# One table of 8 KB rows for U and V, copied in DRAM beside the weight loads, and one gather for both rows of a choice

## The chip, the cores and the metric

One core of a Trainium2 chip runs the whole program. The metric is the device time of one execution in microseconds (us), the median of several runs. Everything is fp32.

## The reference, cut to what matters

A first block of two layers (feed-forward, a mixer, feed-forward each) works on 256 tokens of width 1024; then a second block: an attention mixer, and a feed-forward that picks experts for every token. Only the last part is changed:

```
q = (hc @ w_query)                                # 1024 -> 8 heads x 2 x 128
s = einsum('bthpd,hpnd->bthpn', q, sub_keys)      # scores against 2 x 128 sub-keys of a head
s_top, i_top = top_k(s, 16)
g_s, pos = top_k(all 16 x 16 sums, 16)            # 16 experts of 16384 for each head and token
e_idx = ...                                       # 8 heads x 16 = 128 choices per token
u = u_emb[e_idx]                                  # rows of 1024 floats (4 KB)
act = gelu(einsum('btd,bthkd->bthk', hc, u))
out = einsum('bthk,bthkd->btd', softmax(g_s) * act, v_emb[e_idx])
```

So each of 256 tokens takes 128 rows of U and the same 128 rows of V, 4 KB each: 268.4 MB in all. U and V are inputs of 64 MiB each.

## The kernel before, in words

The order of all work is written out by hand, one program for each engine, with semaphores between them.

**Weights.** Up to the last matrix (`wq`), every weight matrix is streamed in chunks of 2 MiB through two slots of `WR`. SP issues the loads: `load` (L447 on), and for the middle of each feed-forward's `up` matrix the loop in `load_up` (L477). A load waits until DVE has split the last half of the chunk two before it (`lo_ready`). ScalarE (L1293, L1302) copies a half into `WH`, VectorE (L1766, L1781) writes the remainder into `WL`, and TensorE makes three products of each weight. The phases are, in order: up00, down00, kv0, kv1, pool_in, group, pool_outx, pool_out, up01, down01, up10, down10, diff_in, diff_out, up11, down11, in2, out2, wq. GpSimd (POOL) meanwhile loads the 24 MiB matrix `w_ada` in 48 pieces of 512 KB (L529) and reduces them.

**Choices.** VectorE makes the top-16 lists (`choose`, `subkeys`, `gates`) for 16 choices of 128 tokens at a time and signals `index_ready`. Its code interleaves this with the experts' products for the first 128 tokens.

**Experts.** 128 tokens lie on the 128 partitions. The 128 choices of a tile of tokens are 32 groups of `NG` = 4 choices; two tiles give 64 groups. For each group n:

- POOL gathers the four U rows (`gather_u`, L628 on), and the four V rows (`gather_v`, L637 on), with one indirect DMA (L624) per choice and table: 128 rows of 4 KB, 512 KB. Its order is U of group n+1, then V of group n. All four gathers of a group and table count on one semaphore.
- DVE waits for the whole U set, makes four dot products with the token's activations (L2350), then waits for ACT's gelu and multiplies with the gates (L2357).
- ACT makes gelu (L1699) and four diagonal matrices (L1704), double buffered: the diagonals of group n wait for `v_used` of group n-2.
- PE waits for the diagonals and the V set and adds diagonal times V rows in PSUM (L1247), two products for each choice; the last product of a group signals `v_used`.

There are four sets of buffers for U and four for V (`ring`, L100). Two of each (`late_*`) lie over the weight buffers and can be used from group `EARLY` = 6 on, once the last weights are used. U's set comes free with `dots_ready`, V's with `v_used` of the group that used it before. Most of the second tile runs in a hardware loop of four groups.

## Time and profile before

| | |
|---|---|
| median of 3 runs | 2057.4 us (2057.3 to 2062.47) |
| the profiled execution: its own time | 2055.95 us |
| its span, first to last instruction | 2054.4 us |
| busy: PE, DVE, POOL, ACT | 86%, 61%, 44%, 39% of the span |
| moved by DMA | 515.8 MB |
| first gather issued | 1276.8 us from the start |

The busy shares are over the whole span. Up to some 1277 us the weights are streamed, and from there the gathers run; the two parts must be read apart. DMA share in a view is the mean busy share of the core's 16 DMA engines; it can come out a few per cent over 1.

### The profile page before, as it was taken

The page shows a single profiled execution, that of the slowest core. Times are in us where ns is not written, and L with a number is a line of the kernel's source. Part 1 is how long each engine was busy: PE and PEld are TensorE (multiplying, and loading weights), DVE is VectorE, ACT ScalarE, POOL GpSimd, SP SyncE. Part 2 cuts the span into 40 slices and gives each one's busy share as a digit, 9 for nine tenths or more (in the row PEclk, how much of TensorE's full clock was granted, in tenths as well). Part 3 has the DMA queues.
Part 4 walks back from the last instruction along what each step waited for, and adds up shares of the span by engine and source line. Part 5 has one row for each costly group of instructions (what it writes and reads, how often), then busy time and mean ns, then how long its engine had stood idle before and what let it go on. Part 6 is the DMA issues. An engine that isn't in the chain of part 4 may idle for free.

```text
span 2054.4 us, 22931 instructions
## 1 busy us (share of the span) xinstructions
PE 1765.3 (86%) x8110; PEld 1305.6 (64%) x8110; DVE 1261.8 (61%) x2212; ACT 797.1 (39%) x1423; POOL 896.7 (44%) x858
## 2 busy tenths in 40 slices
PE   7999999999999999999989987875675687767677
PEld 6888998888888889888879867642232233223233
DVE  4658756555566567666565847775867776443433
ACT  5444444544544356654443564321222322111112
POOL 5545600362055410115440211556666666666663
PEclk9999999999999999999998998886988799878788
DMA  7775644675576563357563442988999999999995
GB/s 238 247 278 203 213 136 164 205 235 193 184 229 225 195 204 132 139 186 244 205 210 119 151 142 88 348 314 335 373 358 356 355 371 392 374 361 385 355 387 216
DMA packets 248396, 515.80 MB, mean 251 GB/s; under 512 B 16065, under 2 KB 157682, under 8 KB 248306
## 3 DMA queue, kind: packets, MB, share of 16 engines
q0 software_dynamic: 83168, 301.54, 39.7%
q1 hardware_dynamic: 164466, 211.92, 30.8%
q10 hardware_dynamic: 672, 1.18, 0.2%
q8 instruction: 53, 0.87, 0.2%
q14 instruction: 37, 0.30, 0.0%
HBM read 509.34 MB, written 5.26 MB: 250 GB/s over the span
## 4 chain that ended last, share of the span: by engine, by line
PE 62%; issue 25%; DVE 6%; ACT 3%; another core or an unknown queue 2%; DMA 2%; SPq 0%; ACTq 0%; DVEq 0%
PE P L1247 9%; PE PX L789 8%; PE PX L791 8%; PE PX L790 7%; PE P L706 5%; PE P L708 5%; PE P L707 5%; PE P L655 2%; PE P L656 2%; PE P L657 2%; DVE WL L1766 1%; PE P L694 1%; PE P L695 1%; PE P L696 1%
## 5 line engine op out<-in xcount | busy, mean ns | idle before, releaser
L1766 DVE TENSOR_TENSOR WL<-WR,WH 128x1024 fp32r<-128x1024 f32 (+1 forms) x246 | 321.8, 1349 | 191.6 <-ACT WH L1293 191.5
L1293 ACT ACTIVATE WH<-WR 128x1024 fp32r<-128x1024 f32 (+1 forms) x272 | 271.0, 1044 | 324.5 <-PE P L708 150.0
L1247 PE MATMUL P<-early_v,M 128*128 128x512 f32 x544 | 269.0, 653 | 113.3 <-issue 68.6
L1247 PE MATMUL P<-late_v,M 128*128 128x512 f32 x480 | 239.5, 659 | 101.7 <-ACT M L1704 54.8
L789 PE MATMUL PX<-WH,hTh 128*128 128x512 f32 x704 | 279.8, 397 | 5.0 <-DVE WL L1774 4.7
L1247 PEld LDWEIGHTS P<-early_v,M 128*128 128x128 f32 x544 | 112.3, 210 | 265.3 <-issue 218.9
L791 PE MATMUL PX<-WH,hTl 128*128 128x512 f32 x704 | 275.8, 392 | 0.0
L790 PE MATMUL PX<-WL,hTh 128*128 128x512 f32 x704 | 275.0, 391 | 0.0
L1781 DVE TENSOR_TENSOR WL<-WR,WH 128x1024 fp32r<-128x1024 f32 x128 | 177.3, 1426 | 132.0 <-ACT WH L1302 132.0
L1247 PEld LDWEIGHTS P<-late_v,M 128*128 128x128 f32 x480 | 100.6, 213 | 238.8 <-issue 177.2
L624 POOL DMA_INDIRECT early_u<-in_peer_u,M x136 | 131.4, 966 | 152.5 <-DVE M L1989 84.1
L531 POOL TENSOR_TENSOR adaW<-adaW,silc 128x1024 f32<-128x1024 f32 x48 | 100.1, 2086 | 216.4 <-DMA adaW<-in_w_ada 216.4
L1302 ACT ACTIVATE WH<-WR 128x1024 fp32r<-128x1024 f32 x128 | 128.7, 1052 | 159.0 <-PE PX L791 159.0
L706 PE MATMUL P<-WH,actH 128*128 128x512 f32 x472 | 186.6, 395 | 2.0 <-DVE actL L1903 1.0
L708 PE MATMUL P<-WH,actL 128*128 128x512 f32 x472 | 184.1, 390 | 0.0
L707 PE MATMUL P<-WL,actH 128*128 128x512 f32 x472 | 183.8, 389 | 0.0
L1704 ACT ACTIVATE M<-ident,lam 128x128 f32<-128x128 f32 x256 | 81.8, 389 | 260.2 <-remote 190.8
L2350 DVE CUSTOM_DVE_ANT_0 early_u<-early_u,PX 128x1024 f32<-128x1024 f32 x136 | 158.0, 1217 | 25.9 <-DMA early_u<-in_peer_u,M 13.6
L624 POOL DMA_INDIRECT early_v<-in_peer_v,M x136 | 128.9, 948 | 69.2 <-issue 38.7
L789 PEld LDWEIGHTS PX<-WH,hTh 128*128 128x128 f32 x704 | 132.9, 189 | 32.5 <-issue 6.5
L791 PEld LDWEIGHTS PX<-WH,hTl 128*128 128x128 f32 x704 | 132.7, 188 | 28.6
L790 PEld LDWEIGHTS PX<-WL,hTh 128*128 128x128 f32 x704 | 133.0, 189 | 26.7
(367 smaller groups left out, 3330.2 us busy)
## 6 DMA issues: line engine op xcount, KB each, us to landing
WR<-in_ffn_w_up SPq DMA_DIRECT2D x88, 1024.0 KB, 7.4
WR<-in_ffn_w_down SPq DMA_DIRECT2D x44, 1024.0 KB, 6.1
adaW<-in_w_ada POOLq DMA_DIRECT2D x48, 512.0 KB, 4.8
WR<-in_diff_w_in SPq DMA_DIRECT2D x14, 1024.0 KB, 6.9
WR<-in_w_in SPq DMA_DIRECT2D x13, 1024.0 KB, 6.9
WR<-in_mem_w_kv SPq DMA_DIRECT2D x8, 1024.0 KB, 6.7
WR<-in_peer_wq SPq DMA_DIRECT2D x8, 1024.0 KB, 7.3
WR<-in_pool_w_in SPq DMA_DIRECT2D x6, 1024.0 KB, 6.3
```

The source lines that it names most:

```text
L624: pool.indirect_dma_start(rows[:, i, :], None, table, bass.IndirectOffsetOnAxis(ap=eidx[:, at:at + 1], axis=0)).then_inc(landed[i], 16)
L706: mm(o, xh, WH[:, U % 2, w], start=first and kk == 0, stop=False)
L707: mm(o, xh, WL[:, U % 2, w], start=False, stop=False)
L708: return mm(o, xl, WH[:, U % 2, w], start=False, stop=last_half and kk == 1)
L789: mm(o, xh, WH[:, u, w], start=(k == 0), stop=False)
L790: mm(o, xh, WL[:, u, w], start=False, stop=False)
L791: return mm(o, xl, WH[:, u, w], start=False, stop=(k == KT - 1))
L1247: last = mm(P[2 * t + q][:], diag[:, n % 2, i], rows_v(n)[:, i, q * 512:q * 512 + 512], start=n % GROUPS == 0 and i == 0, stop=n % GROUPS ...
L1293: nc.scalar.activation(split_view(WH, U % 2, kind, part), raw(c % 2, kind, h, part), copy)\
L1766: tt(split_view(WL, U % 2, kind, part), raw(c % 2, kind, h, part), split_view(WH, U % 2, kind, part).bitcast(F32), ALU.subtract)\
L1781: tt(split_view(WL, U % 2, "pair", part), raw(c % 2, "pair", h, part), split_view(WH, U % 2, "pair", part).bitcast(F32), ALU.subtract).the ...
L2350: last = nc.vector.tensor_tensor_reduce(out=u[:, i], in0=u[:, i], in1=HTOK[n // GROUPS], scale=1.0, scalar=0.0, op0=ALU.mult, op1=ALU.add, ...
```

## The change

A table `uv_rows` of 16384 rows of 8 KB is made in DRAM, with row e = U's row e, then V's row e. SP copies it there from the two inputs, 128 or 256 rows at a time (one DMA for U, one for V), issued after a chunk's weight loads, in the same queue. Every POOL gather then takes 8 KB rows. The buffers `u` and `v` become one ring of four sets of four choices; each choice has a landing semaphore of its own, and `v_used` counts choices, so that the next gather into a choice's buffer can go once that choice's products are done.

```
+    uv_rows = nc.dram_tensor("uv_rows", (128 * 128, 2 * D), F32, kind="Internal").ap()
+    COPIES = dict(kv0=(1, 1), kv1=(1, 1), pool_in=(1, 1, 1), group=(1,), pool_outx=(1,), pool_out=(1, 1), diff_in=(2,) * 7,
+                  diff_out=(1, 1, 1), in2=(1,) * 7, up00=(0, 0, 0), up01=(1, 1, 1), up10=(1, 1, 1), up11=(1, 1, 1),
+                  down00=(2, 1) * 3, down01=(2, 1) * 3, down10=(2, 1) * 3, down11=(2, 1) * 3)
+    IN_LOOP = (1, 2)
...
+        def copy_rows(at, n):
+
+            for q, table in enumerate((a["peer_u_2"][0], a["peer_v_2"][0])):
+                sp.dma_start(uv_rows[bass.ds(at, n), q * D:q * D + D], table[bass.ds(at, n), :]).then_inc(S["uv_copied"], 16)
+
+        def copy_chunk(name, c):
+
+            n = COPIES.get(name, ())
+            if c < len(n) and n[c]:
+                copy_rows(copy_from[name] + 128 * sum(n[:c]), 128 * n[c])
...
                 load(p["C"] + c)
+                copy_chunk(f"up{i}{f}", c)
...
+                    copy_rows(r * (128 * sum(IN_LOOP)) + (loop_from + 128 * sum(IN_LOOP[:j])), 128 * IN_LOOP[j])
...
+        def gather(n):
+            call = ALL_CALLS.index((n // GROUPS, n % GROUPS * NG // 16))
+            pool.wait_ge(S["index_ready"], call + 1)
+            if n == EARLY:
+                pool.wait_ge(S["half_used"], len(half_of))
             for i in range(NG):
                 at = n * NG + i
...
+                if user_before(n) is not None:
+                    pool.wait_ge(S["v_used"], NG * user_before(n) + i + 1)
+                pool.indirect_dma_start(rows_uv(n)[:, i, :], None, uv_rows,
+                                        bass.IndirectOffsetOnAxis(ap=eidx[:, at:at + 1], axis=0)).then_inc(uv_landed[ring(n)][i], 16)
...
-        gather_u(0)
+        pool.wait_ge(S["uv_copied"], UV_COPIED)
         for n in range(2 * GROUPS):
-            if n + 1 < 2 * GROUPS:
-                gather_u(n + 1)
-            gather_v(n)
+            gather(n)
...
             pe.wait_ge(S["diag_ready"], r * 4 + (n + 1))
-            if n < LAST:
-                pe.wait_ge(v_landed[ring(n)], r * (16 * NG) + turn(n) * 16 * NG)
...
-            last.then_inc(S["v_used"], 1)
+                last.then_inc(S["v_used"], 1)
...
-                act.wait_ge(S["v_used"], r * 4 + (n - 1))
+                act.wait_ge(S["v_used"], r * (4 * NG) + NG * (n - 1))
...
             for i in range(NG):
-                last = nc.vector.tensor_tensor_reduce(out=u[:, i], in0=u[:, i], in1=HTOK[n // GROUPS], scale=1.0, scalar=0.0,
+                dve.wait_ge(uv_landed[ring(n)][i], r * 16 + 16 * turn(n))
+                last = nc.vector.tensor_tensor_reduce(out=u[:, i, 0:D], in0=u[:, i, 0:D], in1=HTOK[n // GROUPS], scale=1.0, scalar=0.0,
                                                       op0=ALU.mult, op1=ALU.add, accum_out=dots[:, g, i:i + 1])
```

`COPIES` gives, for each chunk of a phase, how many times 128 rows are copied behind its load; `IN_LOOP` does so for the eight chunks of an `up` phase's loop. Together they cover the 16384 rows. Phases out2 and wq have none.

## Rows read from the trace of the kernel before

**Rows 1.** The page's 40 slices of 51 us each, TensorE and DMA
```profile
PE   7999999999999999999989987875675687767677
...
DMA  7775644675576563357563442988999999999995
```

**Rows 2.** Waits by engine and line, from 0 to 1277 us
```profile
engine line waited for: us in total, times, longest us
...
DVE WL L1766 <- ACT WH L1293: 186.4, 97, 7.0
ACT WH L1302 <- PE PX L791: 159.0, 64, 3.2
```

**Rows 3.** Busy time by stretch: up00, down00, up01, down01, up10, down10, diff_in, up11, down11, wq
```profile
core 0: us, PE busy (x) PEld busy (x) DVE busy (x) ACT busy (x) POOL busy (x), PEclk, DMA share, GB/s
...
35.00:126.00 91.00, 91.00 (x418) 75.27 (x417) 56.92 (x58) 44.81 (x59) 53.18 (x39) 1.00 0.73 236
126.00:190.00 64.00, 63.01 (x292) 52.08 (x291) 46.74 (x44) 29.20 (x36) 29.24 (x26) 1.00 0.70 256
352.00:463.00 111.00, 110.91 (x512) 91.52 (x512) 68.57 (x77) 58.36 (x79) 48.80 (x40) 1.00 0.68 211
463.00:526.00 63.00, 63.00 (x293) 52.39 (x292) 32.93 (x33) 25.39 (x29) 10.43 (x7) 1.00 0.52 192
530.00:642.00 112.00, 111.88 (x515) 92.34 (x514) 70.58 (x78) 56.94 (x76) 43.33 (x31) 1.00 0.69 221
642.00:703.00 61.00, 61.00 (x286) 50.72 (x285) 36.18 (x34) 26.81 (x32) 25.37 (x18) 1.00 0.61 217
720.00:812.00 92.00, 90.25 (x673) 84.00 (x672) 60.50 (x91) 53.96 (x106) 9.77 (x7) 1.00 0.50 161
892.00:1004.00 112.00, 112.00 (x513) 92.64 (x512) 66.81 (x69) 53.90 (x70) 54.91 (x39) 1.00 0.72 231
1004.00:1055.00 51.00, 51.00 (x238) 42.49 (x237) 28.89 (x24) 19.90 (x22) 24.89 (x18) 1.00 0.59 214
...
1172.00:1277.00 105.00, 85.02 (x607) 75.44 (x605) 62.62 (x110) 54.20 (x114) 13.42 (x18) 0.95 0.37 122
```

**Rows 4.** The same view, three stretches of the gathers
```profile
1277.00:1500.00 223.00, 159.46 (x542) 90.31 (x543) 161.76 (x502) 58.83 (x131) 137.58 (x143) 0.82 0.90 337
1500.00:1740.00 240.00, 168.56 (x347) 70.43 (x345) 175.72 (x463) 58.61 (x140) 157.93 (x168) 0.87 0.96 367
1740.00:2020.00 280.00, 193.19 (x386) 82.24 (x387) 121.68 (x228) 35.89 (x127) 184.96 (x197) 0.80 0.96 370
```

**Rows 5.** Timeline of POOL, 1900 to 1908 us: start, duration, what, idle before
```profile
1900.58 0.94 POOL L624 DMA_INDIRECT early_u<-in_peer_u,M  x1 [0.30 <-issue]
1905.99 0.94 POOL L624 DMA_INDIRECT early_v<-in_peer_v,M  x1 [4.48 <-remote]
1907.24 0.94 POOL L624 DMA_INDIRECT early_v<-in_peer_v,M  x1 [0.30 <-issue]
```

**Rows 6.** Timeline of ACT at the same place
```profile
1905.82 1.28 ACT L1704 ACTIVATE M<-ident,lam 128x128 f32<-128x128 f32 x4 [21.40 <-remote]
```

**Rows 7.** Timeline of PE: the products of one group
```profile
1907.22 16.73 PE L1247 MATMUL P<-late_v,M 128*128 128x512 f32 x32 [10.54 <-issue]
1923.79 7.03 PE L1247 MATMUL P<-early_v,M 128*128 128x512 f32 x16
```

**Rows 8.** Busy time by stretch: one cycle of 34 us, and a dense part of it
```profile
1906.00:1940.00 34.00, 23.60 (x48) 10.11 (x48) 14.45 (x27) 4.18 (x16) 22.57 (x24) 0.80 0.97 369
1930.00:1939.00 9.00, 0.82 (x2) 0.00 (x0) 0.00 (x0) 0.00 (x0) 4.36 (x5) 0.68 1.03 410
```

**Rows 9.** The page's DMA queues: packets, MB, share of 16 engines' span
```profile
q0 software_dynamic: 83168, 301.54, 39.7%
q1 hardware_dynamic: 164466, 211.92, 30.8%
```

**Rows 10.** Busy time by stretch: the one large write to DRAM in progress
```profile
130.00:140.00 10.00, 10.00 (x48) 8.27 (x47) 5.66 (x7) 3.78 (x6) 0.17 (x1) 1.00 1.01 383
```

**Rows 11.** One line's instructions: L477, issues of weight loads on SP (ns min/median/max)
```profile
L477 SPq DMA_DIRECT2D WR<-in_ffn_w_up x64: 372/410/484, 35.5 to 979.9; - x64
```

**Rows 12.** One line's instructions: L2350, the dot products on DVE
```profile
L2350 DVE CUSTOM_DVE_ANT_0 early_u<-early_u,PX x136: 1211/1216/1222, 1290.8 to 2013.1; 128x1024 f32<-128x1024 f32 x136
```

More of the change, by code:

```diff
@@ L89, in program @@
     stage_a.close()
[L91 to L92 removed]
+    late_uv = sb("late_uv", [128, 2, NG, 2 * D])
     late_h = sb("late_h", [128, 2, D])
@@ L96, in program, with rows_uv @@
     htok1 = sb("htok1", [128, D])
[L97 to L98 removed]
+    early_uv = sb("early_uv", [128, 2, NG, 2 * D])
     def ring(n):
         return n % 2 if n < EARLY else n % 4
[L103 to L107 removed]
+    def rows_uv(n):
+        return early_uv[:, ring(n)] if ring(n) < 2 else late_uv[:, ring(n) - 2]
     def turn(n):
@@ L218, in program @@
     raw_landed = [sem("raw_landed0"), sem("raw_landed1")]
-    u_landed = [sem(f"u_landed{i}") for i in range(4)]
-    v_landed = [sem(f"v_landed{i}") for i in range(4)]
-    LAST = 2 * GROUPS - 2
-    last_landed = [[sem(f"last_landed{g}{i}") for i in range(NG)] for g in range(2)]
+    uv_landed = [[sem(f"uv_landed{g}{i}") for i in range(NG)] for g in range(4)]
     b_landed = [sem("b_landed0"), sem("b_landed1")]
@@ L320, in program @@
         slot_loads.append(total[c % 2])
+    COPIES = dict(kv0=(1, 1), kv1=(1, 1), pool_in=(1, 1, 1), group=(1,), pool_outx=(1,), pool_out=(1, 1), diff_in=(2,) * 7,
+                  diff_out=(1, 1, 1), in2=(1,) * 7, up00=(0, 0, 0), up01=(1, 1, 1), up10=(1, 1, 1), up11=(1, 1, 1),
+                  down00=(2, 1) * 3, down01=(2, 1) * 3, down10=(2, 1) * 3, down11=(2, 1) * 3)
+    IN_LOOP = (1, 2)
+    copy_from, copies, at = {}, 0, 0
+    for name in phases:
+        copy_from[name] = at
+        at += 128 * sum(COPIES.get(name, ()))
+        copies += sum(n > 0 for n in COPIES.get(name, ()))
+        if name.startswith("up"):
+            at += 4 * 128 * sum(IN_LOOP)
+            copies += 4 * len(IN_LOOP)
+    assert at == 128 * 128
+    UV_COPIED = 2 * 16 * copies
     block = ctx.enter_context(nc.Block())
@@ L462, in raw_dst_of @@
             return raw_dst(slot, kind, part)
+        def copy_rows(at, n):
[5 more added lines that the diff above has]
+                copy_rows(copy_from[name] + 128 * sum(n[:c]), 128 * n[c])
         def load_up(i, f):
             p = phases[f"up{i}{f}"]
+            loop_from = copy_from[f"up{i}{f}"] + 128 * sum(COPIES[f"up{i}{f}"])
             for c in range(3):
                 load(p["C"] + c)
+                copy_chunk(f"up{i}{f}", c)
                 if i == f == 0 and c == 1:
@@ L483, in _ @@
             else:
-                for c in range(p["C"], p["C"] + p["nc"]):
-                    load(c)
+                for c in range(p["nc"]):
+                    load(p["C"] + c)
+                    copy_chunk(name, c)
         sp.wait_ge(S["index_ready"], len(ALL_CALLS))
@@ L1240, in experts @@
             pe.wait_ge(S["diag_ready"], r * 4 + (n + 1))
-            if n < LAST:
-                pe.wait_ge(v_landed[ring(n)], r * (16 * NG) + turn(n) * 16 * NG)
             for i in range(NG):
-                if n >= LAST:
-                    pe.wait_ge(last_landed[n - LAST][i], 16)
                 for q in range(2):
-                    last = mm(P[2 * t + q][:], diag[:, n % 2, i], rows_v(n)[:, i, q * 512:q * 512 + 512],
+                    last = mm(P[2 * t + q][:], diag[:, n % 2, i], rows_uv(n)[:, i, D + q * 512:D + q * 512 + 512],
                               start=n % GROUPS == 0 and i == 0, stop=n % GROUPS == GROUPS - 1 and i == NG - 1, skip_group_check=True)
-            last.then_inc(S["v_used"], 1)
+                last.then_inc(S["v_used"], 1)
         for j in range(8):
@@ L2385, in add_experts @@
         def add_experts(t):
-            dve.wait_ge(S["v_used"], t * GROUPS + GROUPS)
+            dve.wait_ge(S["v_used"], NG * (t * GROUPS + GROUPS))
             if t:
```

29 lines of the change are left out of this document (2 added, 27 removed).

## The prediction, made before the changed kernel ran

> **What bounds the kernel now.** I read the page's slices first [rows 1]. They show two programs in one. Up to about the 25th slice (1277 us) TensorE's digit is 9 nearly everywhere while DMA's lies between 3 and 7; after it DMA's is 8 or 9 and TensorE's 5 to 7. The waits of the first part [rows 2] say the same: the splitting engines wait for each other and, in the end, for TensorE to free a buffer; no wait for a weight load stands high. So weights arrive early, and TensorE sets the pace. In the second part the stretches [rows 4] show DMA at a share of 0.90, 0.96 and 0.96, moving 337, 367 and 370 GB/s. The gathers set the end.
>
> How much is left there? The timeline from 1900 us on shows a cycle. POOL issues gathers every 1.245 us (0.94 and 0.30 idle), then stops once for 4.48 us [rows 5]; ACT, which needs the same count `v_used` for its diagonals, stands 21.4 us and is released at the same moment [rows 6]; PE idles 10.54 us [rows 7]. One cycle is 34 us and three groups, 24 gathers [rows 8]: 24 x 1.245 + 4.48 = 34.4. In the dense part the engines move 410 GB/s at a share of 1.03, over the cycle 369 [rows 8]. So a tenth of the rate is lost after each stop. POOL cannot make it good: 524 KB in 1.245 us is 421 GB/s, hardly more than the 410 that DMA takes. Why the count comes so late the trace doesn't say.
>
> **The copies.** They move 128 x 2 x 512 KiB = 134.2 MB. COPIES and IN_LOOP make 93 calls, so 186 more DMAs on SP, in its queue between weight loads. At the 0.41 us of a load's issue [rows 11] that is 76 us of SP, which otherwise only waits for slots; on a chunk's path stand two issues, 0.8 us, before the wait for the next slot. TensorE's time for a chunk is about 11 us (112 us of a stretch with some ten chunks, [rows 3]), so SP hides it. What counts is the data: a load queues behind the copy that was issued before it.
>
> What does a byte copied from DRAM to DRAM cost? No such transfer of any size is in the trace. The nearest rows from one side: a gather reads DRAM at 410 GB/s and share 1.03 [rows 8], the store of `rel_rows` writes to DRAM among loads at 383 GB/s in total and share 1.01 [rows 10]. If a DMA engine reads and writes at once, the copy costs what a gather costs: 398 GB/s per unit of share. From the other side: if reading and writing DRAM take turns, each byte costs twice, 199. No reason excludes either; I take the first, since a gather too is a read and a write in each packet and the rows of either direction are near each other. The range keeps both.
>
> Room is (1.03 minus share) times length, stretch by stretch [rows 3], against the copies' need at 398:
> - up00: 27.3 us of room, 12.6 MB need 31.6, over by 4.3. down00: 21.1, 9.4 MB need 23.7, over by 2.6.
> - up01: 38.9, 15.7 MB need 39.5: 0.6. down01: 32.1, need 23.7: none.
> - up10: 38.1: 1.4. down10: 25.6: none. diff_in: 48.8, 14.7 MB need 36.9: none.
> - up11: 34.7: 4.8. down11: 22.4: 1.3.
>
> Sum 15 us. The other phases have room. For copies that come in lumps of 1 and 2 MiB (2.6 and 5.3 us) before a load, I add 0.1 us for each of the 68 feed-forward chunks: 22 us in all. The wait of gather 0 for the copies costs nothing: after in2 comes wq without copies, 105 us at share 0.37 [rows 3]. If the copies ran beyond that, every gather would be late.
>
> The Trainium skill has a rule that speaks against this. "DMA: Bandwidth & Descriptors", section "Latency and other measured facts", gives 214 GB/s per direction as the full rate of copies between tensors in HBM. By that figure, an estimate, the copies would take 627 us of all engines, near the second case above; no run here shows it yet.
>
> **The gathers.** Bytes stay 268.4 MB; 512 gathers become 256.
> - *Packets.* q0 took 0.397 x 16 x 2054.4 / 83168 = 156.9 ns per packet of 3626 bytes, q1 61.6 ns per 1288 bytes [rows 9]. A straight line through both has 9.1 ns per packet. 32768 packets fewer on 16 engines: 18.6 us. I take 18. The other bound is nothing, if a row of 8 KB is cut in two. The same page of the Trainium skill, section "SWDGE vs HWDGE vs iDMA", wants packets of at most 4096 bytes; by that rule these 18 us would be gone.
> - *POOL.* At 0.94 + 0.30 us for an instruction of 1 MB it could issue 842 GB/s, and refill the queues after a stop. If a row makes two descriptors, an instruction may cost 2.5 us, and POOL stays at 421: then this gain is nothing.
> - *Late stretch*, 1740 to 2020: at 410 instead of 370, 280 x (1 - 370/410) = 27. I take 20, since the late count's cause isn't known and may remain; the bounds are 0 and 27.
> - *Middle*, 1500 to 1740: 240 x (1 - 367/410) = 25. DVE is busy 73% there with the choices of the second tile, and buffers come free only behind it. I take half, 13; bounds 0 and 25.
> - *Early*, 1277 to 1500: 40 us are lost at 337 GB/s, but two sets of buffers until wq ends and the first top lists make that, and both stay. I take 4; bounds 0 and 15.
>
> The buffers are the same bytes. U's set was free after the dot products, now it waits for PE: against that each choice is freed alone. DVE now waits for each choice, and the sorting of later choices is queued behind that wait; the dots of a group take 4 x 1.22 = 4.9 us [rows 12] of 10.2 us that 4 MB need at 410 GB/s. PE needs 7.03 us for a group [rows 7], also under 10.2. PE's own wait for V goes, since the diagonal comes from the same landing. These edits cost nothing while DMA is the slower one. The end, from the last landing on, is one dot, gelu, diagonals and seven us of PE as before: nothing.
>
> Gain 18 + 20 + 13 + 4 = 55. Against the profiled execution's own 2055.95 us: + 22 - 55 = 2023. The median of the runs is 1.5 us above it: 2024.
>
> **The rivals.**
> - *The copies starve TensorE.* Place: the queue of SP in the up and down phases. With 199 GB/s the needs double: over by 36, 26, 40, 15, 41, 22, 25, 44 and 25 us in the order above, 275 together, less 55: about 2277. At 300 GB/s at share 1.03 (reads and writes hinder each other in part) I get 97, so 2099. It decides from where the overload passes 55 us, some 330 GB/s. For it: no free room in four up phases even at the best rate. Against it: TensorE has two halves split ahead, and `w_ada`'s loads can give way. The result is slower.
> - *The gathers gain little.* If the rate is what DRAM gives for scattered rows and rows of 8 KB are cut, and the late counts remain, 0 to 15 us are won and 15 to 22 paid: about 2063. For it: 410 is seen as a ceiling everywhere. Against: the loss of a tenth is plain in the cycle.
> - *More is won.* With POOL far ahead the early and middle stretches also reach 410 and the copies cost nothing: 2055.95 - 18 - 27 - 25 - 15, about 1973.
> - *It doesn't do what it says:* the table isn't complete at 1277 and gather 0 waits. This is part of the first rival, since FIFO order makes the last copies late only if the loads are late too.
>
> **Chances.** Forecast 0.42. Copies starve TensorE: 0.37, of it 0.19 near half rate and 0.18 between. Gathers gain little 0.15, of it 0.07 within 0.3%, 0.06 slower and 0.02 faster. More is won 0.06. That makes faster 0.50, same 0.07, slower 0.43; 0.3% (6 us) is about what a measurement of this kernel can tell from no change. The likeliest case's own range is 1990 to 2050. For 8 in 10 the range reaches from 1975 up to 2200: it leaves out the worst of the copies at about half rate, some 0.15, and a little below. It is wide since cases of both signs hold most of the chance.
>
> **What the profile would show.** TensorE at 9 up to 1277 us with DMA near full in the up phases, and gather 0 still near 1277 to 1300: the copies' step is right. Waits of ACT for DMA of `WR` of more than 30 us in total, or a first gather after 1340: the first rival. In the gathers: 256 instructions of about 0.94 us on POOL, with long waits for buffers between them, and a rate near 410 GB/s in the last stretch. Packets of q0 down by about 32768 prove rows of one packet; if they stay, the 18 us are wrong. ACT's waits of 20 us gone: the late count was tied to the old waits. If they stay and the rate still rises, the refill did it. The prediction is wrong if copies run below 330 GB/s or the rate of the gathers stays below 385.

## The result, and the profile after

The changed kernel takes 2008.15 us (median of 4 runs, 1992.75 to 2009.55) against 2058.89 (4 runs of the kernel before, 2057.3 to 2062.47) in the same comparison: ratio 0.9729, interval 0.9707 to 0.9752. That is faster by 51 us, well beyond the 6 us that a measurement can tell from nothing. The forecast said 2024. On another chip (e6 below) the same change is slower than the kernel before, by 28 us; so this number belongs to the chip that it was measured on.

The profiled execution took 2008.95 us with a span of 2007.4 (before: 2055.95 and 2054.4). One instant splits it in two: the first gather starts at 1320.40, where it was 1276.8. Up to there the change costs 43.6 us. From there to the end of the span it takes 687.0 us instead of 777.6, and wins 90.6. The net of the two is the 47 us between the spans. The forecast had 22 and 55.

The page of the changed kernel, its slices of 50 us (the GB/s row is what moved in each):

```profile
PE   7999999999999999999999789788688877778776
...
DMA  8999976799899989758998656368999999999995
GB/s 268 326 373 381 305 257 252 261 348 373 290 313 347 373 282 337 259 206 306 330 335 300 201 193 204 105 256 328 420 420 420 420 420 419 420 421 421 421 421 224
```

DMA's digit, 2 to 7 before the gathers [rows 1], is mostly 7 to 9 now where copies run, while TensorE keeps its 9 in most slices. From the 29th slice on the rate stands at 419 to 421 GB/s in every slice but the last. That flat row is what the change won: no stop, no slow recovery after one.

The same page, its DMA part: packets by size, the two large queues (packets, MB, share of 16 engines' span), and issues (KB each, median us from issue to landing):

```profile
DMA packets 247274, 649.99 MB, mean 324 GB/s; under 512 B 14945, under 2 KB 156562, under 8 KB 214418
...
q1 hardware_dynamic: 200210, 346.15, 50.4%
q0 software_dynamic: 46304, 301.52, 37.6%
...
WR<-in_ffn_w_up SPq DMA_DIRECT2D x88, 1024.0 KB, 9.9
WR<-in_ffn_w_down SPq DMA_DIRECT2D x44, 1024.0 KB, 11.1
uv_rows<-in_peer_u SPq DMA_DIRECT2D x35, 1024.0 KB, 13.5
```

- q0 fell from 83168 packets [rows 9] to 46304, by 36864: 32768 for the rows, and 16 small ones for each of the 256 gathers that are gone. Of all packets 247274 - 214418 = 32856 have 8 KB or more: each gathered row of 8 KB went as one packet.
- q1 grew by 35744 packets and 134.2 MB, the copies. The time of all its packets grew by 0.504 x 16 x 2007.4 - 0.308 x 16 x 2054.4 = 6063 us, so 170 ns for a packet of 3755 bytes: with 16 engines 354 GB/s. That puts the whole growth down to the copies. Against the 398 GB/s of a gather [rows 8] a copied byte costs an eighth more, not double.
- A load of `w_up` lands after 9.9 us and one of `w_down` after 11.1. In the trace of the kernel before these were 7.4 and 6.1.

Busy time by stretch, changed kernel (columns as in [rows 3]; the stretches are those of [rows 3] and [rows 4], five of the feed-forward phases and three of the gathers, the last one ended before the drain):

```profile
126.00:190.00 64.00, 60.97 (x280) 49.77 (x279) 40.35 (x41) 26.63 (x33) 23.47 (x23) 1.00 1.00 384
463.00:526.00 63.00, 60.32 (x272) 49.35 (x271) 34.80 (x34) 24.87 (x31) 21.86 (x16) 0.97 0.93 343
530.00:642.00 112.00, 111.87 (x512) 92.03 (x511) 68.51 (x75) 55.30 (x73) 29.07 (x21) 1.00 0.98 317
642.00:703.00 61.00, 56.30 (x259) 46.21 (x258) 36.54 (x35) 25.79 (x33) 28.45 (x20) 0.97 1.02 370
892.00:1004.00 112.00, 109.67 (x500) 89.70 (x499) 71.87 (x73) 56.09 (x76) 30.46 (x22) 0.98 0.91 303
1277.00:1500.00 223.00, 175.14 (x755) 113.24 (x754) 184.83 (x550) 74.51 (x159) 66.25 (x68) 0.88 0.82 324
1500.00:1740.00 240.00, 192.56 (x397) 79.99 (x395) 189.35 (x491) 65.21 (x156) 94.58 (x100) 0.91 1.01 420
1740.00:1970.00 230.00, 177.99 (x365) 73.53 (x366) 117.53 (x211) 34.10 (x115) 82.68 (x89) 0.93 1.01 420
```

The middle and the late stretch went from 367 and 370 GB/s to 420, at a share of 1.01 (416 GB/s per unit of share; 4 KB rows gave 398). In up10 TensorE still has 111.87 of 112 us, in up11 109.67 where it had 112.00. In the down phases it idles: 60.32 of 63 us in down01 and 56.30 of 61 in down10, where it had 63.00 and 61.00.

The gathers gain in all their stretches, the first included. By 1500 us the kernel before had moved 73.0 MB of rows, 223 us after its first gather; the changed kernel had them after 194. The last 100 us of that stretch, first of the kernel before, then of the changed one:

```profile
1400.00:1500.00 100.00, 61.30 (x118) 25.66 (x119) 66.82 (x212) 22.24 (x51) 62.44 (x67) 0.80 0.91 347
1400.00:1500.00 100.00, 70.34 (x148) 30.52 (x149) 92.57 (x310) 31.80 (x72) 36.92 (x39) 0.84 1.01 420
```

Waits by engine and line (us in total, times, longest), changed kernel, 0 to 1300 us:

```profile
POOL adaW L554 <- DMA adaW<-in_w_ada: 343.3, 48, 10.1
...
ACT WH L1309 <- DMA WR<-in_ffn_w_up: 64.1, 13, 7.1
...
ACT WH L1300 <- DMA WR<-in_ffn_w_down: 38.0, 9, 6.0
```

No wait for a weight load stood high before [rows 2]. Now ACT stands 64.1 + 38.0 us for `WR` in these two lines, and 145 us over all matrices against 24 before. Part of it reaches TensorE: those are its idle microseconds in the down phases.

The same view from 1300 us on, then POOL's timeline (start, duration, what, idle before and who ended it) and the gathers as one line's instructions (ns min/median/max, first and last start):

```profile
ACT lam L1706 <- DVE lam L2357: 471.8, 64, 9.5
...
POOL early_uv L651 <- PE P L1254: 182.9, 111, 15.2
POOL late_uv L651 <- PE P L1254: 182.2, 108, 7.6
...
DVE early_uv L2357 <- DMA early_uv<-uv_rows,M: 82.3, 69, 3.2
```

```profile
1320.40 1.77 POOL L651 DMA_INDIRECT early_uv<-uv_rows,M  x1 [76.00 <-DVE M L1996]
...
1346.74 0.94 POOL L651 DMA_INDIRECT early_uv<-uv_rows,M  x1 [15.23 <-PE P L1254]
```

```profile
L651 POOL DMA_INDIRECT early_uv<-uv_rows,M x136: 932/936/1768, 1320.4 to 1940.3; - x136
L651 POOL DMA_INDIRECT late_uv<-uv_rows,M x120: 932/936/1183, 1393.5 to 1960.2; - x120
```

256 instructions of 0.936 us issue the 256 gathers of 1 MB, and POOL waits 365 us for buffers in between: it is far ahead of the DMA engines. ACT's single waits of 21.4 us [rows 6] are gone; its longest is 9.5. The first gather waited for DVE's index, not for the copies.

### The profile page after: what moved, and what is told of

It reads as the page before. It is cut to its first block, busy times and chain, and to the rows that moved or that the text cites. A ratio compares the mean times of both kernels' runs of the same rounds, so it can differ in the third digit from the quotient of the medians.

```text
span 2007.4 us, 22993 instructions
## 1 busy us (share of the span) xinstructions
PE 1774.0 (88%) x8110; PEld 1306.8 (65%) x8110; DVE 1277.5 (64%) x2212; ACT 795.6 (40%) x1423; POOL 652.1 (32%) x602
## 2 busy tenths in 40 slices
DMA packets 247274, 649.99 MB, mean 324 GB/s; under 512 B 14945, under 2 KB 156562, under 8 KB 214418
## 3 DMA queue, kind: packets, MB, share of 16 engines
q0 software_dynamic: 46304, 301.52, 37.6%
## 4 chain that ended last, share of the span: by engine, by line
PE 39%; DMA 28%; DVE 16%; POOL 8%; ACT 4%; issue 4%; SPq 0%; ACTq 0%; DVEq 0%; POOLq 0%
DMA late_uv<-uv_rows,M 12%; DMA adaW<-in_w_ada 10%; PE P L1254 6%; PE P L717 3%; PE P L718 3%; PE P L719 3%; PE PX L800 3%; DVE WL L1773 3%; DMA early_uv<-uv_rows,M 3%; PE PX L802 3%; PE PX L801 3%; POOL adaW L554 2%; POOL adaW L555 2%; DVE early_uv L2357 2%; PE P L666 2%
## 5 line engine op out<-in xcount | busy, mean ns | idle before, releaser
L1254 PE MATMUL P<-early_uv,M 128*128 128x512 f32 x544 | 260.4, 635 | 56.2 <-ACT M L1711 56.2
L1254 PE MATMUL P<-late_uv,M 128*128 128x512 f32 x480 | 240.8, 660 | 78.0 <-ACT M L1711 78.0
L1788 DVE TENSOR_TENSOR WL<-WR,WH 128x1024 fp32r<-128x1024 f32 x128 | 185.1, 1486 | 135.8 <-ACT WH L1309 135.7
L1254 PEld LDWEIGHTS P<-late_uv,M 128*128 128x128 f32 x480 | 99.4, 213 | 218.2 <-issue 117.7
L1254 PEld LDWEIGHTS P<-early_uv,M 128*128 128x128 f32 x544 | 108.0, 203 | 204.5 <-issue 133.6
L651 POOL DMA_INDIRECT early_uv<-uv_rows,M x136 | 130.1, 956 | 286.2 <-PE P L1254 182.9
L2357 DVE CUSTOM_DVE_ANT_0 early_uv<-early_uv,PX 128x1024 f32<-128x1024 f32 x136 | 162.5, 1220 | 85.5 <-DMA early_uv<-uv_rows,M 82.3
L1706 ACT ACTIVATE lam<-lam 128x4 f32<-128x4 f32 x64 | 13.1, 205 | 471.8 <-DVE lam L2357 471.8
L2357 DVE CUSTOM_DVE_ANT_0 late_uv<-late_uv,PX 128x1024 f32<-128x1024 f32 x120 | 143.4, 1220 | 76.4 <-DMA late_uv<-uv_rows,M 75.8
L651 POOL DMA_INDIRECT late_uv<-uv_rows,M x120 | 113.4, 945 | 187.1 <-PE P L1254 182.2
## 6 DMA issues: line engine op xcount, KB each, us to landing
WR<-in_ffn_w_down SPq DMA_DIRECT2D x44, 1024.0 KB, 11.1
WR<-in_diff_w_in SPq DMA_DIRECT2D x14, 1024.0 KB, 11.6
```

Source lines behind the costliest of these rows:

```text
L651: pool.indirect_dma_start(rows_uv(n)[:, i, :], None, uv_rows, bass.IndirectOffsetOnAxis(ap=eidx[:, at:at + 1], axis=0)).then_inc(uv_landed ...
L1254: last = mm(P[2 * t + q][:], diag[:, n % 2, i], rows_uv(n)[:, i, D + q * 512:D + q * 512 + 512], start=n % GROUPS == 0 and i == 0, stop=n ...
L1788: tt(split_view(WL, U % 2, "pair", part), raw(c % 2, "pair", h, part), split_view(WH, U % 2, "pair", part).bitcast(F32), ALU.subtract).the ...
L2357: last = nc.vector.tensor_tensor_reduce(out=u[:, i, 0:D], in0=u[:, i, 0:D], in1=HTOK[n // GROUPS], scale=1.0, scalar=0.0, op0=ALU.mult, op ...
```

## The experiments

Questions: what do the copies cost, and where; what of the gathers' gain comes from long rows, from the ring released per choice, and from the vanished stops. The kernels of one series ran on one chip, with the kernel before beside them. The four series ran on four chips, and that turned out to matter most. No chip was used in two of them, so a condition of the chip at that hour is not told from the chip itself; within a series no run of the kernel before was of the other kind.

### First series: e1 to e4, the kernel before at 1979.3 us

The expectations were written against a kernel before of about 2057 us. On this chip it took 1979.3 (17 runs, 1977.26 to 1981.78). So only the ratios and the differences within the series can be read.

**e1_no_copies.** The gathers of 8 KB rows without copies:

```
-    uv_rows = nc.dram_tensor("uv_rows", (128 * 128, 2 * D), F32, kind="Internal").ap()
+    uv_rows = a["peer_u_2"][0].rearrange("(a b) n -> a (b n)", b=2)
     ...
-                sp.dma_start(uv_rows[bass.ds(at, n), q * D:q * D + D], table[bass.ds(at, n), :])...
+                pass
     ...
-        pool.wait_ge(S["uv_copied"], UV_COPIED)
     ...
-            stt(eidx[:, at:at + 16], ps[:, 0], float(128), ps[:, 1], ...
+            stt(eidx[:, at:at + 16], ps[:, 0], float(63), ps[:, 1], ...
```

> The changed kernel without its copies: the gathers take rows of 8 KB from U read as a table of 8192 rows, with indices 63 a + b instead of 128 a + b, so V's half and the output are other numbers, while bytes, row size and waits stay. Theory A (the 44 us by which the first gather comes later, 1320 against 1277, are all the copies' cost, and the gathers don't care where the table came from): first gather near 1277, time near 2008 - 44 = 1964. Theory B (part of the delay comes from the new order of gathers, which wait for PE while only two sets are free): first gather at 1277, but a gather part longer than the 687 us of the changed kernel, time 1970 to 1990.

Measured: 1976.35 us (1972.3 to 1977.8), ratio 0.9981 (0.9972 to 0.9991). First gather at 1278.84, steady rate 420 GB/s, span 1974.1, so 695.3 us of gathers, 8.8 more than in e6 below, where the indices are the true ones. They arise ahead of the 25th gather, the first of group 6, which is issued 82.5 us after the first against 72.8 in e6; what caused them wasn't found. Long rows alone, without any cost for making them, are worth 3 us on this chip. The gain of 90 us that the first comparison showed wasn't there to be won.

**e2_two_gathers.** The changed kernel's ring and its release per choice, but two gathers of 4 KB rows, no copies:

```
-                pool.indirect_dma_start(rows_uv(n)[:, i, :], None, uv_rows, ...)
+                for q, table in enumerate((a["peer_u_2"][0], a["peer_v_2"][0])):
+                    pool.indirect_dma_start(rows_uv(n)[:, i, q * D:q * D + D], None, table, ...)
     ...
-                dve.wait_ge(uv_landed[ring(n)][i], r * 16 + 16 * turn(n))
+                dve.wait_ge(uv_landed[ring(n)][i], r * 32 + 32 * turn(n))
```

> No table and no copies; the ring, the landing count per choice and the release per choice as in the changed kernel, but each choice fetched by two gathers of 4 KB rows, from U and from V. Theory rows (the gathers' gain of 91 us comes from 8 KB rows: one packet instead of two, and a POOL that is far ahead): the gather part stays near the 778 us of before, less only a little, time 2030 to 2055. Theory waits (it comes from the waits per choice, which end the cycle of 34 us): dense gathers at 410 GB/s as in the dense part of before, gather part near 687 x 420/410 = 704, time near 1981.

Measured: 1985.43 us (1984.28 to 1986.96), ratio 1.0034 (1.0023 to 1.0044), at 409 to 410 GB/s from the 29th slice on. First gather 1279.87, span 1984.0, gathers 704.1 us. The ring with its waits costs 6 us here instead of the nothing that I had put down. The loss is at the end, not in the waits for buffers: from the first gather to the last one's issue it takes 660.4 us, in e5 below 659.4, but from there to the end of the span 43.7 against 37.8. The last dot product and the last products of TensorE, first of e5 (the kernel before on a chip of this kind), then of e2:

```profile
1957.12 1.22 DVE L2350 CUSTOM_DVE_ANT_0 late_u<-late_u,PX 128x1024 f32<-128x1024 f32 x1
1955.62 13.90 PE L1247 MATMUL P<-late_v,M 128*128 128x512 f32 x32
```

```profile
1966.02 1.22 DVE L2357 CUSTOM_DVE_ANT_0 late_uv<-late_uv,PX 128x1024 f32<-128x1024 f32 x1 [1.30 <-DMA late_uv<-in_peer_v,M]
1969.23 7.13 PE L1254 MATMUL P<-late_uv,M 128*128 128x512 f32 x16 [1.34 <-ACT M L1711]
```

In e5 the dots of the last group are done while V is still on its way, and TensorE then works without a gap up to 7.6 us before the end of the span. In e2 the last dot itself waits for the last landing, and gelu, diagonals and products stand behind it, again up to 7.6 us before the end.

**e3_group_release.** The changed kernel, but the dots start when all four choices of a group have landed, and POOL waits for a whole group's buffers:

```
-                if user_before(n) is not None:
-                    pool.wait_ge(S["v_used"], NG * user_before(n) + i + 1)
+                if i == 0 and user_before(n) is not None:
+                    pool.wait_ge(S["v_used"], NG * user_before(n) + NG)
     ...
                 dve.wait_ge(uv_landed[ring(n)][i], r * 16 + 16 * turn(n))
+            for i in range(NG):
```

> The changed kernel with its table, but buffers released by the group (the first gather of a group waits for all four choices of the group before) and dot products that start when all four rows have landed. Theory rows: no difference, time 2005 to 2012, as the queue is deep enough. Theory waits: the cycle with a drained queue comes back at least in part, 2025 to 2050.

Measured: 2021.21 us (2016.23 to 2025.17), ratio 1.0212 (1.0191 to 1.0234). The changed kernel itself took 2006.8 on another chip of the same kind (e6, below). So the release per choice and the dots per choice, which this run takes away together, are worth some 14 us; its rate from 1500 us on is 418 to 420 GB/s either way, and the loss is ahead of 1500 us, where two sets of buffers have to do (308 GB/s from 1277 to 1500, against 335 in e6).

**e4_copies_only.** The kernel before with all the copies, which nothing reads but a wait for their count ahead of the first gather. The added lines are those of the change (`COPIES`, `copy_rows`, `copy_chunk` and their calls) and

```
+        pool.wait_ge(S["uv_copied"], UV_COPIED)
         gather_u(0)
```

> The kernel before with the copies into the table, which nobody reads; the gathers are those of before and wait for the copies as in the changed kernel. If the copies alone cost what the later first gather shows: first gather near 1320, time near 2058 + 44 = 2102. If the copies only cost together with the new gathers, less.

Measured: 2016.28 us (2014.14 to 2022.34), ratio 1.0197 (1.018 to 1.0215). First gather at 1312.58, which is 32.7 us after that of e2 on the same chip. Copies alone cost 37 us. They are a cost of the weight part; the gathers then run at 408 to 410 GB/s, as without them.

### Second series: e5 to e8, the kernel before at 1978.8 us

Was the first series' chip odd, and does the change lose there? The two kernels as they are, e2 again, and a first remedy for the copies.

**e5_before_again.** No edit.

> The kernel before, unchanged, beside which the first experiments ran at 1979 us on their chip, 79 us below the 2058 of the comparison. Theory chip (the cycle of 34 us with its 21 us waits for v_used appears on some chips only): a profile either with the cycle and about 2058, or without it, gathers steady at 409 GB/s, and about 1979. Theory drift (it is a passing condition of one execution): runs of both kinds in one series.

Measured: 1979.36 us (1977.42 to 1981.22), ratio 1.0003 (0.9994 to 1.0013). Its page, the rate by slice, and two stretches of [rows 4] (columns as there):

```profile
GB/s 239 250 282 192 206 157 171 181 216 236 171 212 220 199 223 171 128 144 203 247 209 213 86 161 144 82 360 369 409 409 409 409 409 409 410 410 410 409 410 262
```

```profile
1277.00:1500.00 223.00, 180.17 (x609) 98.58 (x609) 198.11 (x605) 68.56 (x155) 156.14 (x163) 0.90 0.98 378
1500.00:1740.00 240.00, 186.01 (x369) 76.39 (x368) 164.84 (x411) 57.83 (x145) 181.80 (x192) 0.89 1.03 409
```

It is the same program as in the rows ahead of the prediction. The weight part takes the same time (first gather 1279.87 against 1276.8). But the cycle of [rows 8] isn't there: 409 GB/s all along instead of 367 and 370, and the gathers take 697.2 us instead of 777.6. The 80 us between the chips are the cycle, which holds from the start of the gathers: 378 against 337 GB/s up to 1500 us.

**e6_after_again.** No edit to the changed kernel.

> The changed kernel, unchanged, on the same chip as the kernel before. Theory chip: where the kernel before has the cycle, about 2008 against 2058, ratio 0.973; where it has none (1979), the copies' 40 us stand against some 15 us of faster gathers, so about 2008, ratio 1.012 to 1.017. If instead the gain belongs to the 8 KB rows everywhere, the ratio is 0.973 here too.

Measured: 2006.81 us (2003.14 to 2008.22), ratio 1.0146 (1.0129 to 1.0163): on this chip the change is slower, by 28 us, which is 1.5%, and the interval leaves out 1. First gather 1315.14, span 2001.6, gathers 686.5 us. The changed kernel takes the same time on both kinds of chip (2008.15 and 2006.81); the kernel before doesn't.

**e7_two_gathers_again.** The kernel of e2.

> The ring and the waits per choice, with two gathers of 4 KB rows and no copies, again. On a chip without the cycle 1985 as before. On a chip with the cycle: theory waits (the waits per choice end it) 1985; theory rows (8 KB rows end it) 2040 to 2060.

Measured: 1985.73 us (1983.64 to 1986.81), ratio 1.0036 (1.0022 to 1.0051), as in e2.

**e8_copies_later.** Six units of copies (of 128 rows of U and of V) are moved out of the last two down phases into phases behind, `out2` and `wq` among them:

```
-                  diff_out=(1, 1, 1), in2=(1,) * 7, up00=(0, 0, 0), ...
-                  down00=(2, 1) * 3, down01=(2, 1) * 3, down10=(2, 1) * 3, down11=(2, 1) * 3)
+                  diff_out=(2, 1, 1), in2=(1,) * 7, out2=(1, 1), wq=(1, 1, 1), up00=(0, 0, 0), ...
+                  down00=(2, 1) * 3, down01=(2, 1) * 3, down10=(1,) * 6, down11=(1,) * 6)
```

> The changed kernel with six of the 128 copy units moved out of down10 and down11, the two phases that the changed kernel's trace shows 10 us late each, into diff_out (one), out2 (two) and the first three chunks of wq. Theory room (a phase is late by as much as its copies exceed DMA's room): down10 and down11 late by 3 us each instead of 10, time 10 to 15 us below the changed kernel. Theory backlog (the lateness comes from lumps anywhere): no gain, or the late copies hold up the weights of wq, within 4 us of it.

Measured: 2001.42 us (1996.19 to 2006.08), ratio 1.0108 (1.0082 to 1.0133). From the first load of `down10` to that of the next phase it takes 71.3 us, of `down11` 72.0; in e6 76.9 and 76.9, in e5 68.6 and 68.5. So those phases do pay for their copies, by 8 us each, and a third less copying there takes most of it away. The profiled execution, at 2006.08, is the slowest of the four and shows only 1.7 us of gain at the first gather; the median gains 5.4, where 10 to 15 were expected. down01, whose copies stayed, took 11.7 us more than in e5 (9.1 in e6), and wq with its new copies 3.4 more.

### Third series: e9 and e10, the kernel before at 2057.4 us

Is it the amount of copies in the down phases, or that they come in lumps (2, 1, 2, 1)? This chip has the cycle again.

**e9_downs_light.** All four down phases at one unit a chunk, twelve units moved behind:

```
-                  diff_out=(1, 1, 1), in2=(1,) * 7, up00=(0, 0, 0), ...
-                  down00=(2, 1) * 3, down01=(2, 1) * 3, down10=(2, 1) * 3, down11=(2, 1) * 3)
+                  diff_out=(2, 1, 1), in2=(2,) * 6 + (1,), out2=(1, 1), wq=(1, 1, 1), up00=(0, 0, 0), ...
+                  down00=(1,) * 6, down01=(1,) * 6, down10=(1,) * 6, down11=(1,) * 6)
```

> The changed kernel with one copy unit (1 MiB) behind every chunk of the four down phases instead of 2, 1, 2, 1, 2, 1: twelve units of 128 moved, six of them as before into diff_out, out2 and wq, six more into in2. So far a down phase is 8 to 10 us late with 9 units (3 us with 6), and the up phases hardly. Theory room: four down phases late by about 3 us instead of 8, in2 by 3 us more, first gather near 1295 to 1300 against 1315, time 1988 to 1994. Theory backlog (each unit costs the same wherever it stands): first gather near 1313, time near 2004.

**e10_even_lumps.** The same amount in each down phase as in the change, in even portions of 192 rows:

```
-                  down00=(2, 1) * 3, down01=(2, 1) * 3, down10=(2, 1) * 3, down11=(2, 1) * 3)
+                  down00=(1.5,) * 6, down01=(1.5,) * 6, down10=(1.5,) * 6, down11=(1.5,) * 6)
```

> The changed kernel with the same bytes in every phase, but the down phases' copies even: 1.5 MiB behind each of six chunks instead of 2, 1, 2, 1, 2, 1. Theory lumps (a weight load stands too long behind a copy of 2 MiB): the down phases late by 3 us instead of 8, time near 1990. Theory room (the bytes of a phase count, not their order): no difference, 2004 to 2009.

Measured: e9 1989.24 us (1985.13 to 1993.42), ratio 0.9663 (0.9635 to 0.969); e10 2004.67 us (2002.03 to 2009.43), ratio 0.9744 (0.9712 to 0.9775), about the change's own 0.9729. First gathers 1305.65 and 1317.23. Two down phases, down01 and down10, busy time by stretch, first of e9, then of e10:

```profile
463.00:526.00 63.00, 58.57 (x257) 48.00 (x257) 30.10 (x32) 22.79 (x28) 23.06 (x16) 0.95 0.79 288
642.00:703.00 61.00, 57.74 (x266) 47.52 (x265) 35.15 (x35) 24.45 (x32) 28.57 (x21) 0.97 0.98 342
```

```profile
463.00:526.00 63.00, 58.45 (x263) 47.92 (x262) 30.69 (x33) 23.54 (x28) 24.13 (x16) 0.97 0.88 329
642.00:703.00 61.00, 56.97 (x261) 46.64 (x260) 37.40 (x36) 25.61 (x33) 28.29 (x20) 0.97 1.00 358
```

Even portions change nothing; less in these phases brings the first gather 11.6 us forward, where 15 to 20 were expected. `down01` is no better for it: it moves only 288 GB/s at a share of 0.79, and TensorE is no busier there than in e10.

Where TensorE falls behind can be read by taking the same product of TensorE (the n-th of 8110) in two traces. How much later it starts than in the kernel before (for e6, than in e5), by the time t at which it starts there:

| t in the kernel before, us | 470 | 515 | 660 | 740 | 1000 | 1045 | 1270 |
|---|---|---|---|---|---|---|---|
| changed kernel | 6.2 | 11.0 | 11.3 | 24.4 | 30.2 | 39.2 | 43.0 |
| e6, the same | 5.3 | 13.8 | 13.6 | 24.8 | 24.8 | 31.2 | 34.7 |
| e9 | 5.2 | 13.3 | 13.7 | 21.6 | 21.6 | 25.1 | 28.2 |
| e10 | 5.6 | 12.3 | 12.6 | 24.5 | 24.4 | 36.9 | 39.8 |

From 470 to 515 us TensorE has the end of up01 and the first chunks of down01; from 515 to 660 the rest of down01 and nearly all of up10; from 660 to 740 the entry into down10, down10 and the entry into diff_in; from 1000 to 1045 the entry into down11. These three short stretches hold 26.9, 26.1, 19.5 and 31.1 us of the lag at the end. The rest of down01 and up10, whose chunks have their copies too, cost at most 0.4 us in any of the four. The waits of ACT for a weight load around down01, first of the changed kernel (its third is of 1.11 us, at 497), then all of e9:

```profile
471.82 2.01 ACT L1300 ACTIVATE WH<-WR 128x1024 fp32r<-128x1024 f32 x2 [4.09 <-DMA WR<-in_ffn_w_up]
485.09 2.01 ACT L1300 ACTIVATE WH<-WR 128x1024 fp32r<-128x1024 f32 x2 [5.99 <-DMA WR<-in_ffn_w_down]
```

```profile
470.09 2.01 ACT L1300 ACTIVATE WH<-WR 128x1024 fp32r<-128x1024 f32 x2 [3.32 <-DMA WR<-in_ffn_w_up]
483.94 2.01 ACT L1300 ACTIVATE WH<-WR 128x1024 fp32r<-128x1024 f32 x2 [5.81 <-DMA WR<-in_ffn_w_down]
```

The late loads are those of up01's last chunk and of down01's first. In both kernels these were issued behind the copies of up01's last chunks, which e9 left as they were, and landed 9 to 16 us after their issue; the loads of down01 from the fourth chunk on landed after 5 to 9. Entry and rest of down01, of the changed kernel and of e9:

```profile
470.00:505.00 35.00, 32.32 (x156) 26.39 (x155) 20.33 (x22) 15.06 (x19) 16.17 (x14) 1.00 1.02 388
505.00:535.00 30.00, 30.00 (x127) 24.65 (x126) 10.84 (x11) 9.71 (x10) 1.80 (x2) 0.94 0.81 284
```

```profile
470.00:505.00 35.00, 30.57 (x145) 24.93 (x143) 20.97 (x20) 15.14 (x19) 17.82 (x14) 0.98 0.91 341
505.00:535.00 30.00, 30.00 (x124) 24.74 (x125) 9.71 (x10) 8.05 (x8) 2.31 (x2) 0.91 0.58 213
```

The share of 0.79 is a mean of two stages, 0.91 and 0.58. After its idle time TensorE is busy all the time, but at a granted clock of 0.94 and 0.91, where the kernel before had 1.00 in the same stretch. In the trace these are 3.4 us from 505.4 on and, in e9, 6.8 us from 503.9 on at the lower level (1.2 GHz), with 2.4 GHz around them; so some 2 and 3 us of the lag are the clock. What e9 wins over e10 it wins at the entry into down11 (3.5 us for 12.5) and from 660 to 740 us (7.9 for 11.9). Why nothing comes of it at down01 stays open, and a kernel without copies behind the last chunks of the up phases wasn't run. e9 beats the kernel before, and e10 beside it, on a chip with the cycle. It wasn't run on one without.

### Fourth series: e11 and e12, the kernel before at 2055.8 us

What ends the cycle: the release per choice, the new ring with its waits, or the long rows?

**e11_release_per_choice.** The kernel before, with V's buffers released choice by choice:

```
-        def gathers(rows, table, landed, n):
+        def gathers(rows, table, landed, n, used=False):
             for i in range(NG):
                 at = n * NG + i
+                if used and user_before(n) is not None:
+                    pool.wait_ge(S["v_used"], NG * user_before(n) + i + 1)
     ...
-            last.then_inc(S["v_used"], 1)
+                last.then_inc(S["v_used"], 1)
```

> The kernel before with one edit: v_used is signalled for each choice and V's gathers wait for their own choice; U, the order of the gathers and the landing counts stay. It tells something where the kernel before runs at 2057. Theory release (one late v_used stops POOL and ACT together; counted by the choice it can't): 1980 to 1990. Theory order or landing (the cycle hangs on U before V, or on four gathers that share a count): 2040 to 2057. Where the kernel before runs at 1979, it stays within 5 us of that and tells nothing of the cycle.

Measured: 2071.9 us (2069.57 to 2074.17), ratio 1.0081 (1.006 to 1.0101). Two stretches of e11, and its waits from 1740 to 2000 us:

```profile
1500.00:1740.00 240.00, 158.49 (x323) 66.20 (x322) 168.77 (x452) 53.94 (x129) 149.12 (x159) 0.84 0.92 347
1740.00:2020.00 280.00, 190.69 (x398) 81.13 (x397) 119.45 (x225) 38.31 (x129) 185.60 (x199) 0.84 0.98 373
```

```profile
ACT M L1704 <- remote: 125.2, 7, 25.0
```

The stops stay, with waits of up to 25 us by ACT for `v_used`, and the kernel is 16 us slower than the kernel before. The release alone doesn't end them.

**e12_two_gathers_third.** The kernel of e2 and e7, on a chip with the cycle.

> The changed kernel's ring and waits with two gathers of 4 KB rows and no copies, a third time. It tells something where the kernel before runs at 2057: theory waits (ring and waits per choice alone end the cycle) 1985, so 22 us below the changed kernel; theory rows (only 8 KB rows and the POOL that is far ahead end it) 2040 to 2057.

Measured: 2060.36 us (2057.05 to 2066.84), ratio 1.0023 (1.0008 to 1.0039). Its middle and late stretch and two of its waits from 1740 to 2000 us; then the late stretch of the same kernel in e2, on the chip without the cycle:

```profile
1500.00:1740.00 240.00, 173.01 (x351) 72.38 (x350) 181.67 (x479) 63.62 (x151) 158.62 (x168) 0.86 0.97 366
1740.00:2020.00 280.00, 188.31 (x386) 79.65 (x385) 125.12 (x226) 34.79 (x121) 184.71 (x197) 0.82 0.97 370
```

```profile
ACT lam L1706 <- issue: 96.0, 11, 14.9
...
ACT M L1711 <- remote: 66.5, 5, 14.7
```

```profile
1740.00:1940.00 200.00, 155.08 (x315) 63.16 (x314) 99.27 (x176) 29.65 (x100) 147.44 (x158) 0.92 1.03 410
```

366 and 370 GB/s are, within 1 GB/s, the numbers of [rows 4] again. The kernel is otherwise that of the change: same ring, same waits, same order of work. Only the rows are of 4 KB, from the two inputs, with two instructions for a choice, and there are no copies. So neither the ring nor its waits keep the cycle away; the long rows of the table do, with half as many gather instructions and packets. Row length and number of instructions went together in every kernel here, and weren't told apart. Nor was e1, with 8 KB rows out of an input and no copies, run on a chip with the cycle. That the place of the table in DRAM, or the copies, end the cycle is therefore not excluded; against the copies stands that the last one had landed at 1214 us, 107 us ahead of the first gather.

## Why the prediction was right, and where it was off

The side, the number (2024 for 2008) and the range held, on this chip. The nearness of the number is in part luck: the cost was put 22 us too low and the gain 36 us too low, and the two misses have opposite signs. Point by point:

- **Rate of a copy: right in kind, an eighth too high.** 170 ns per packet of 3755 bytes, 354 GB/s. I had 398 from the gathers. The bound of half that rate is excluded. By the figure that I had quoted from the Trainium skill ("DMA: Bandwidth & Descriptors", "Latency and other measured facts", 214 GB/s per direction) 134 MB would be an estimate of 627 us. The 134.2 MB took 6063 us of packet time, 379 us for each of 16 engines: the measurement doesn't agree, and it decides.
- **Issue of the copies: mis-sized, 76 us for 270.** Each of the 186 issues of copies on SP took longer than a load's 0.41 us, one of them 7.5. The two lines of L475 (ns min/median/max) are these. SP had the time for it in the up phases, which grew by 2.1 us in all in e6 (table below).

```profile
L475 SPq DMA_DIRECT2D uv_rows<-in_peer_u x93: 511/1347/7507, 35.1 to 1202.7; - x93
L475 SPq DMA_DIRECT2D uv_rows<-in_peer_v x93: 522/599/2068, 36.9 to 1203.8; - x93
```

- **Cost of the copies: mis-sized, 22 for 43.6 us.** The step that failed is "down01, down10, diff_in: none". My overloads come to 15.0 us, and 6.8 more were for the chunks' loads behind a copy. Below is by how much each group of phases grew, from the first load of each phase on SP; the last column is e6 less e5, on the chip without the cycle.

| phases | forecast overload | this comparison | e6 less e5 |
|---|---|---|---|
| up00, up01, up10, up11 | 11.1 | 11.1 | 2.1 |
| down00, down01, down10, down11 | 3.9 | 27.1 | 29.7 |
| all others, up to the first gather | 0 | 5.4 | 3.5 |

  The up phases were right, or too dear. The down phases weren't. The first load of a phase is issued some two chunks before TensorE uses it, so a down row also holds the end of the up phase ahead of it. The cost arises there, at the entry into a down phase. Its loads stand behind the last copies of the up phase and the first of its own; in down01 they landed up to 17 us after their issue (the median of all `w_down` loads went from 6.1 to 11.1 us), while a chunk lasts some 10.5 us (63 us, six chunks). The room that I had counted is a mean over the stretch: down01 had 8.4 us of room to spare and still grew by 3.0 us here and by 9.1 in e6. My 0.1 us a chunk for that was far too little. Nor would the measured rate have mended the working: with 354 for 398 the same sums give 41 us, near the 43.6, but 30 of them in the up phases, where 11.1 were measured. e10 excludes the uneven portions as the cause; e8 and e9 say that a third less copying in the down phases gives back 10 us of 16.5 in down10 and down11 (e8), and over all four phases 10 of 27 (e9, against the changed kernel).

- **The wait of gather 0 for the copies: nothing, as forecast.** DVE's index released it after 76.00 us, with the last copy issued before `wq` began.
- **Packets: right.** 32856 packets of 8 KB or more, q0 down by 36864 (the 32768 that I had, and 4096 small ones). At steady state 409.5 became 420 GB/s: 268.4 MB take 639.1 instead of 655.5 us, 16.4 for my 18. From the Trainium skill's preference for packets of at most 4096 bytes ("DMA: Bandwidth & Descriptors", "SWDGE vs HWDGE vs iDMA") I had that these 18 us might be gone; rows of 8 KB went as one packet and were 2.6% faster here.
- **POOL: right.** 0.936 us for an instruction of 1 MB, 365 us of waits for buffers.
- **Late and middle stretch: right in kind, too small.** I took 20 of 27 and half of 25, for fear that the late count stays. It went altogether, and both stretches run at 420, for the same bytes 30 and 34 us less, of which 5 to 6 each are the packets'.
- **Early stretch: wrong.** I took 4 us, with 15 as the bound, since two sets of buffers seemed to make the 337 GB/s. The same 73.0 MB took 29 us less. On the chip without the cycle the kernel before had 378 GB/s there with the same two sets: most of what I had put down to the buffers was the cycle. This stretch has some 20 of the 36 us between 55 and 90.6.
- **Ring and waits "cost nothing", the end "as before": wrong by some 7 us.** e2's gathers take 704.1 us against 697.2 of e5 at the same rate, and 5.9 of the 6.9 lie behind the issue of the last gather: the dots of the last group now wait for the last landing, where U had landed ahead of V. The release per choice, which I had only as a counterweight, is worth at most 14 us, by e3 and with the dots per choice.

The gathers' gain can be told in two parts. On the chip without the cycle it is 697.2 - 686.5 = 10.7 us, of which the steps above make 16.4 - 6.9 = 9.5. What is left of the 90.6, 80 us, is the difference of the kernel before between the two chips, 777.6 - 697.2 = 80.4.

The **rivals**. "The copies starve TensorE" came true in part: ACT's waits for `WR` are 102 us where I had named 30 as the mark, but the rate stayed above the 330 GB/s from which it decides. "The gathers gain little" holds on the chip of e6 by its amount, a gain of 10.7 us and a cost of 35.3, though not by its reason, since the rows weren't cut; and there the change is slower, an outcome of that case to which I had given 0.06. So the forecast was right for the mechanism it read in its own trace, a tenth of the rate lost after each stop. I hadn't thought that this loss could belong to the chip, and none of my rivals says so.

**Open:** why the count `v_used` comes late on some chips. It isn't the granularity of the release alone (e11) nor the ring and its waits (e12), and on the other chips the same instructions in the same order don't show it. Why long rows end it is argued, not shown: in [rows 5] POOL's 421 GB/s is hardly above what DMA takes, so after a stop of 4.48 us nothing is in reserve, while 842 GB/s refills the queues. A kernel with 8 KB rows and POOL held to one instruction each 2.5 us would have tried that; it wasn't tried.

## What to carry to other kernels

A stop-and-recover cycle in a trace may belong to the chip: before a change is paid for with 40 us elsewhere, run the kernel before on more than one chip and see that the loss is there each time. What background copies cost isn't told by a phase's mean room: here most of it arose at the change from one phase to the next, where loads stood behind the last copies of the phase ahead. To find the place, take the same product in two traces and see where it falls behind. That thinning the copies just there pays wasn't tried. Where the engine that issues gathers is hardly faster than the DMA engines that serve them, longer rows pay by the packet, and perhaps a second time by the reserve, which wasn't shown.

## What the runs showed of the hardware that I had not expected

- The kernel before took 2055.8 to 2058.9 us in three of the comparisons and 1978.8 and 1979.3 in two others, the runs of one series within 0.6%. The granted clock in the weight part and its length are the same; only the gathers of 4 KB rows differ, 370 against 409 GB/s. With rows of 8 KB both kinds give 420.
- Copies from DRAM to DRAM and weight loads together reached 384 GB/s at a share of 1.00 (126 to 190 us), nearly the rate of loads with one large write, 383 at 1.01 [rows 10].
- A row of 8 KB was moved as one packet, at 416 GB/s per unit of share; rows of 4 KB gave 398.
- A short idle time of TensorE was followed by a lower granted clock: 30.57 us busy of 35 in e9's entry into down01, then 6.8 us at the lower level (1.2 GHz) while it was busy throughout; the kernel before had 35.00 of 35 there and no such stretch.
